# Row loads by panel, row stores held back, and the squares of queries and keys on ScalarE, in a hybrid decoder layer

## What is computed

```
hn = rmsnorm(h, g_attn_norm)
z = hn @ w_in                                  # 1280 columns: q (8 heads of 64), k and v (2 heads), u (512)
q = rmsnorm(q.reshape(B, S, 8, 64), g_q)       # per head: sum of 64 squares
k = rmsnorm(k.reshape(B, S, 2, 64), g_k)
a = sliding_window_sink_attention(q, k, v, sinks, rel_bias)    # window 128, blocks of 128
m = multiscale_pool_mixer(u, w_pool, pool_scale)
h = h + concatenate([a, m]) @ w_out
h = h + (silu(rmsnorm(h) @ w_gate) * (rmsnorm(h) @ w_up)) @ w_down
h = h + sigmoid(rmsnorm(h) @ w_ple_gate) * (p @ w_ple_proj)
```

## Time and profile before

| | |
|---|---|
| median of 3 runs | 2043.66 us (2039.48 to 2045.55) |
| the profiled execution, its own time | 2043.7 us |
| its span, first to last instruction | 2041.9 us |
| PE busy in it | 2014.0 us, 99% |
| DVE / ACT / POOL busy | 1377.4 / 900.8 / 394.6 us |
| mean granted TensorE clock | 0.998 |
| moved by DMA | 292.10 MB, 143 GB/s over the span |

### The profile page before, as it was taken

The page is one execution under the profiler, slowest core; times in us unless marked ns, Lnnn a source line. Parts: engine busy times, 40 slices in busy tenths (PEclk is TensorE's granted clock), DMA queues, the critical chain, the costliest instruction groups (busy, mean ns, idle before and its releaser), DMA issues.

```text
span 2041.9 us, 26161 instructions
## 1 busy us (share of the span) xinstructions
PE 2014.0 (99%) x9565; PEld 1665.5 (82%) x9565; DVE 1377.4 (67%) x1936; ACT 900.8 (44%) x1461; POOL 394.6 (19%) x502
## 2 busy tenths in 40 slices
PE   9999999999999999999999999999999999999998
PEld 7887878877888888888888888788888888888887
DVE  4686664767695655655888765966566566987763
ACT  5684744757433333333433543533333333334542
POOL 5443644543410000000000220000000000001210
PEclk9999999999999999999999999999999999999999
DMA  8658566364934223225825129432322328342143
GB/s 205 196 176 268 186 237 201 130 239 149 354 110 138 71 70 108 73 68 177 302 63 164 36 74 231 135 119 73 95 82 71 101 78 291 136 151 82 47 134 103
DMA packets 195488, 292.10 MB, mean 143 GB/s; under 512 B 14661, under 2 KB 116429, under 8 KB 194080
## 3 DMA queue, kind: packets, MB, share of 16 engines
q1 hardware_dynamic: 172672, 212.97, 34.4%
q0 software_dynamic: 22544, 77.46, 11.2%
q10 hardware_dynamic: 144, 0.00, 0.0%
HBM read 223.25 MB, written 67.51 MB: 142 GB/s over the span
## 4 chain that ended last, share of the span: by engine, by line
PE 85%; DVE 5%; DMA 4%; issue 2%; ACT 2%; POOL 1%; SPq 0%; ACTq 0%; DVEq 0%; POOLq 0%
PE bank L2642 13%; PE bank L2646 13%; PE bank L2644 13%; PE bank L2681 7%; PE bank L2680 7%; PE bank L2679 7%; PE bank L2341 5%; PE bank L2343 5%; PE bank L2342 5%; PE bank L2317 2%; PE bank L2319 2%; PE bank L2318 2%; DMA w_parts<-w_split 1%; PE bank L2410 1%; DMA raw<-in_w_ple_gate 1%
## 5 line engine op out<-in xcount | busy, mean ns | idle before, releaser
L2642 PE MATMUL bank<-a_hi,ring_hi 128*128 128x512 f32 x1232 | 479.7, 389 | 1.1 <-DVE ring_lo L1936 0.7
L2644 PE MATMUL bank<-a_lo,ring_hi 128*128 128x512 f32 x1232 | 479.3, 389 | 0.0
L2646 PE MATMUL bank<-a_hi,ring_lo 128*128 128x512 f32 x1232 | 479.3, 389 | 0.0
L2642 PEld LDWEIGHTS bank<-a_hi,ring_hi 128*128 128x128 f32 x1232 | 231.2, 188 | 50.0 <-DVE ring_lo L1936 1.4
L2646 PEld LDWEIGHTS bank<-a_hi,ring_lo 128*128 128x128 f32 x1232 | 231.2, 188 | 48.1
L2644 PEld LDWEIGHTS bank<-a_lo,ring_hi 128*128 128x128 f32 x1232 | 231.2, 188 | 47.8
L2679 PE MATMUL bank<-d_hi 128*128 128x512 f32 x616 | 239.8, 389 | 0.0
L2681 PE MATMUL bank<-d_hi,d_lo 128*128 128x512 f32 x616 | 239.7, 389 | 0.0
L2680 PE MATMUL bank<-d_lo,d_hi 128*128 128x512 f32 x616 | 239.6, 389 | 0.0
L1402 ACT ACTIVATE d_hi<-keep 128x1024 fp32r<-128x1024 f32 x132 | 139.8, 1061 | 201.9 <-PE bank L2681 184.9
L2066 DVE TENSOR_TENSOR d_lo<-keep,d_hi 128x1024 fp32r<-128x1024 f32 x132 | 164.2, 1246 | 52.8 <-ACT d_hi L1402 52.6
(11 more groups left out here) (271 smaller groups left out, 3879.8 us busy)
## 6 DMA issues: line engine op xcount, KB each, us to landing
w_parts<-w_split POOLq DMA_DIRECT2D x88, 512.0 KB, 4.9
hidden_T<-hid POOLq DMA_DIRECT2D x88, 256.0 KB, 2.3
raws<-in_w_gate SPq DMA_DIRECT2D x80, 256.0 KB, 4.7
raws<-in_w_up SPq DMA_DIRECT2D x80, 256.0 KB, 5.1
keep<-hidden_T SPq DMA_DIRECT2D x66, 256.0 KB, 3.6
raw<-in_w_ple_gate SPq DMA_DIRECT2D x64, 256.0 KB, 4.1
keep<-in_w_down SPq DMA_DIRECT2D x44, 256.0 KB, 4.1
other<-hidden_T SPq DMA_DIRECT2D x44, 256.0 KB, 7.0
```

The costliest lines, as they stand in the source:

```text
L2642: mm(dst[:, :], wh[:, g, cols], a_hi[o][:, k, :], start=fresh and k == 0, stop=False, skip_group_check=True)
L2644: mm(dst[:, :], wh[:, g, cols], a_lo[o][:, k, :], start=False, stop=False, skip_group_check=True)
L2646: ins = mm(dst[:, :], wl[:, g, cols], a_hi[o][:, k, :], start=False, stop=k == 3, skip_group_check=True)
```

## The change

Three edits. `store_h1(t-1)`, which stands at the fourth panel in SP's list of `z_section(t+1)`, first waits until PE has done two panels of that section (tiles 2 and 3 of the z sections; the store after the third tile is as before). In `out_section(1)` SP's four chunk loads and four row loads, which all stood at the first panel, are issued in three portions: chunks 0 and 1 at the first; chunks 2 and 3 and the rows b = 0 and 1 when panel 38 is done; the rows b = 2 and 3 when panel 39 is done. The squares of queries and keys stay on POOL in tile 0 and are made by ACT in tiles 1, 2 and 3, in the same halves, ahead of the hosted attention step.

```
                     if t and c == 3:
+                        sp.wait_ge(panel_used, Z_AT[t + 1] + 2)
                         store_h1(t - 1)
...
                     load_out(t, c)
-                    if t == 1 and c == 0:
-                        for k in range(4):
+                    if t == 1 and c < 3:
+                        if c:
+                            sp.wait_ge(panel_used, OUT_AT[1] + c)
+                        for k in ((0, 1), (2, 3), ())[c]:
                             load_chunk(3, k)
-                        for b in range(NB):
+                        for b in ((), (0, 1), (2, 3))[c]:
                             load_h(1, b)
...
-                    if half in QK_SQUARES_AT.get(t, {}):
+                    if t == 0 and half in QK_SQUARES_AT[0]:
                         squares_qk(t, QK_SQUARES_AT[t][half])
...
+            def squares_qk(s, b):
+                n = 4 * s + b
+                act.wait_ge(kvcopied, n + 1)
+                if n:
+                    act.wait_ge(qred, n)
+                nc.scalar.activation(qk_sq[:, :], qkv_of(s)[:, b, 0:QKW], ACT.Square).then_inc(qsq, 1)
...
                     if t >= 2 and half == SPREAD2_AT + 1:
                         copy_spread2(t - 2, bank[6])
+                    if t and half in QK_SQUARES_AT.get(t, {}):
+                        squares_qk(t, QK_SQUARES_AT[t][half])
                     hosted("z", t, half)
```

## The result

The changed kernel takes 2049.41 us (median of 7 runs, 2048.80 to 2049.82) against 2042.94 for the kernel before, run on the same chip (7 runs, 2039.48 to 2045.55): a ratio of 1.0033 with a 95% interval of 1.0024 to 1.0043, so 6.5 us slower. Forecast were 2042.0 and a range up to 2048.0; the time lies 1.4 us above the range. The profiled execution took 2049.19 of its own.

What follows compares the result with a forecast made beforehand. PE, busy 2014.0 of 2041.9 us, bounds the kernel, so only pauses and slow clock could change. 2043.7 - 1.3 - 4.8 + 0.3 + 0.3 - 1.0 + 0.6 + 1.6 + 2.7 = 2042.1, said as 2042; range 2036.3 to 2048.

Steps and rivals of the forecast that it cites:

- the second +0.3 of the sum: Out part of tile 1, panel 42: additions wait for late rows and chunk 4, costing 0.3 us, bounds 0 and 3.
- The second rival: The load wait only moves, to panel 40 or panel 42's additions: 3.15 plus 1.7 slow clock, 2046.3 us; chance 0.17.
- The held store: Second panel of tile 2, at 216.42: PE's wait for weights goes, gain 1.3 us, bounds 0 and 1.3.
- Panel 39: At 300.37: PE's 3.15 us wait for weights and 1.7 of slow clock disappear, gain 4.8 us.
- Panel 40: Needed at 303.3, landing between 302 and 304.5 beside the moved loads: stall of 0.3 us, bounds 0 and 1.2.
- VectorE freed of the square: Tile 2, at 270.53: VectorE no longer meets a GpSimd square, PE's pause at 275.05 goes, gain 1.0 us.
- The squares on ScalarE: Tiles 1, 2 and 3: in-order squares waiting for sums delay attention steps, costing PE 0.6, 1.6 and 2.7 us.
- The third rival: Tiles 1 to 3: each square's wait on the sums costs PE a full turn, 22 us, giving 2059; chance 0.11.
- the first: Rival: ScalarE's waits in tiles 1 to 3 cost nothing and the other gains stay, 2036.7 us; chance 0.17.

Runs made afterwards that it cites:

- The fifth kernel: Changed kernel, but chunks 0 to 3 loaded at once, chunks 4 and 5 before the wait for panel 38, only rows by panel: 2042.82 us, ratio 1.0003.
- the sixth: Changed kernel, loads untouched, but VectorE does the additions ahead of the remainders of chunks 4 and 5 in halves 6 and 7: 2045.29 us, ratio 1.0018.

## Why the prediction was wrong

**The step that failed** is the second +0.3 of the sum: "Chunk 4, behind `load_h` in SP's list, is now held by these waits too and lands near 312 ... So I take another 0.3, bounds 0 and 3." The mechanism stood there in full, place and order included. The size was off: chunk 4 landed at 318.6, not 312, and the pause was 5.73 with 2.4 of slow clock behind it, 8.3 in all. The rows, put at 311 to 312 in the same working, landed at 316.6, by which PE would have waited 2.6 without any chunk. Two things were left out. I timed the landing with the 7.7 us of the earlier trace rows, while the moved loads came into engines kept full from 302 to 317, with panels 41 to 43 beside them (rows 10.5, chunk 4 13.4). And I gave the term no slow clock, though I had worked out 1.7 for the same thing at panel 39. The second rival had both, at 3.15 and 1.7 and a chance of 0.17, and ended at 2046.3; this is the way it went, at a higher price. The fifth kernel shows it (6.6 us back by the order of issues alone), the sixth splits it, 3.1 for the wait for chunk 4 in VectorE's order and 2.6 for the rows.

**The held store**, -1.3: the wait went, 1.6 gained at 216, but 1.1 came back at 230, where VectorE, now early, met GpSimd. Net -0.5. I had asked what waits for the store, not what an earlier PE would meet next, though I had the same collision in hand at 270.53.

**Panel 39**, -4.8: measured -5.0, 3.3 for the pause and 1.7 for the clock. Right in the pair of traces compared; but that the kernel before loses the 1.7 in each execution was taken for granted. With the held store alone the same panel made PE wait 3.27 us and the clock did not fall.

**Panel 40**, +0.3: nothing in the kernel after. But the step was right only by luck, by the company it had: with the squares on GpSimd the same loads wait 5.29 there, beyond the bound of 1.2. I gave the panel 1.5 us nearly alone; it had 2.6 in the one and 0.6 in the other.

**VectorE freed of the square**, -1.0: measured -1.1, the pause at 275 is gone.

**The squares on ScalarE**, +0.6, +1.6 and +2.7: measured +0.8, +1.7 (1.9, less 0.2 that came back by 295) and +3.1, pause by pause where they were put. The third rival, a full turn for each wait, and the first, nothing, are both out. The kernels with two buffers and with the square behind the step confirm the cause, since either one takes away most of the pauses of tiles 2 and 3.

**The sum of the measured terms** is -1.6 + 1.1 - 5.0 + 0 + 8.3 - 1.1 + 0.8 + 1.7 + 3.1 = +7.3, against -1.6 forecast. The kernel's medians differ by 6.5. Of the 8.9 of error 8.0 are the term of panel 42 and 0.8 that of the held store; the rest cancels to 0.1. These terms add up since they are read from one pair of traces. Made alone, the parts give +0.2 (squares) and +0.8 (loads and stores), together +6.5: each part alone wins back much of the same stall at panel 39 (3.6 and 5.0), which can be had only once.

Not settled: whether moving GpSimd's additions would save the gain of the held store was not tried, so that collision rests on the fourteen traces alone; and why the feed-forward part takes up to 3.4 us more or less from trace to trace was not looked into.

## What to carry to other kernels

When a load is put behind a wait in an in-order queue, list everything behind it in that queue, and for the first of these follow the landing through every engine that handles it, at the landing time of full DMA engines, with the slow clock that may follow as a term with a chance of its own: 1.5 to 2.9 us behind seven of the nine pauses of 2.6 to 5.7 us here. Issue what another engine needs first ahead of the waiting load: here that alone was 6.6 us. On a kernel that is 99% PE a gain is often a pause that moves, so ask what the earlier engine meets next, and test parts in combination, for one part may pay out of the stall that another is to remove, or keep another's loads in front.

## What the runs showed of the hardware

**Two queues share the DMA engines about evenly, but only after a delay.** Packets, MB and share of 16 engines by queue in the kernel before, first over 290 to 295, then over 295 to 300.3:

```profile
q1 hardware_dynamic: 454, 1.60, 93.2%
q0 software_dynamic: 16, 0.07, 3.5%
...
q0 software_dynamic: 304, 1.11, 57.7%
q1 hardware_dynamic: 410, 1.00, 50.4%
```

and in the kernel with only loads and stores, over 302 to 307.4:

```profile
q1 hardware_dynamic: 290, 1.06, 53.5%
q0 software_dynamic: 292, 1.07, 53.4%
```

In the prediction I read the 1.05 MB in 10 us of panel 39 as a third of the flow, and set that against the even split. It is next to nothing in the first 5 us and half in the rest. The Trainium skill (DMA: Bandwidth & Descriptors, Queues, rings and completion order) has a DMA engine go round between its queues packet by packet, which I took for an even split; the later stretches agree, 1.11 against 1.00 and 1.07 against 1.06 MB, and the first does not. Why GpSimd's load, issued at 290.10 behind 3 MB of SyncE's, moved 0.07 MB by 295 stays open. In the kernel after, with the engines idle, the same load, issued at 288.88, had moved 0.45 MB by 292. In the kernel with only loads and stores 1.57 MB of GpSimd's queue had gone by (0.50 from 297 to 302, 1.07 from there to 307.4) before panel 40, 1.05 MB, was complete: panel 41, issued directly behind it, took part of the half. That reading is argued, not measured.

**The clock behind a pause.** Behind PE pauses of 2.62, 3.15, 3.20, 3.56, 3.97, 5.29 and 5.73 us the granted clock of the next stretches fell, a part of them at 1.2 GHz (to 0.73, 0.66, 0.77, 0.50, 0.50, 0.57 and 0.52). The first three cost 1.5 to 1.7 us each, the other four 2.5 to 2.9. Behind two others it did not fall: 2.56 us (two buffers) and 3.27 us, with the held store alone, at panel 39:

```profile
300.44 0.47 PE L2342 MATMUL bank<-mix_hi,w_parts 128*128 128x512 f32 x1 [3.27 <-DMA w_parts<-w_split]
```

```profile
300.00:305.00 5.00, 4.56 (x20) 3.82 (x21) 0.00 (x0) 0.00 (x0) 0.00 (x0) 1.00 1.08 387
```

Here 20 matmuls run in the stretch that has 13 in the kernel before, behind a pause that was 0.12 us shorter. So the length of the pause alone does not tell whether the clock falls, and the 1.7 us are not lost in every execution.

**One instruction under GpSimd, in two places.** The same `mix_lo` takes 0.42 to 0.43 us alone and 1.43 to 1.50 where a GpSimd instruction lies over it, at 227 to 231 for GpSimd's additions as at 270 to 274 for its squares.
